# Retention's gated product ahead of its rounding, and two orders in the first block, in a two-block model kernel

## The reference, cut to what matters

```python
# first block, HGRN2 mixer: forget gate and its running sums, attention with decays between positions
fgate = lb + (1.0 - lb) * sigmoid(f);  log_f = log(fgate)
diff = bb[:, :, :, None, :] - bb[:, :, None, :, :]
decay = exp(where(mask, diff, -inf))
att = einsum('bhtd,bhsd,bhtsd->bhts', qq, kk, decay)
x = x + concatenate([y_a, y_b, y_c, y_d]) @ w_out
# second block, both layers
o = _rms((inner + cross)) * silu(gate)            # retention, 4 chunks of 128 positions
mixed = g[:, :, 0] * o_a + g[:, :, 1] * o_b + g[:, :, 2] * o_c    # g: sigmoids of a product with h
x = x + mixed @ w_out
```

## Time and profile before

| | |
|---|---|
| median of 3 runs | 2644.86 us (2643.98 to 2648.19) |
| profiled execution | 2648.18 us, its span 2646.3 us |
| TensorE busy | 2585.7 us, 98% |
| VectorE busy | 1453.3 us, 55% |
| ScalarE busy | 678.7 us, 26% |
| GpSimd busy | 1490.1 us, 56% |
| mean granted TensorE clock | 0.994 |

### The profile page before, as it was taken

One profiled execution on the slowest core, in us unless ns is written; L12 is line 12 of the kernel. 1 busy time (PEld: TensorE's weight loads), 2 busy tenths in 40 slices (PEclk: granted clock), 3 DMA queues, 4 the chain that ended last, 5 costly groups with the idle time before them and its releaser, 6 DMA issues.

```text
span 2646.3 us, 47390 instructions
## 1 busy us (share of the span) xinstructions
PE 2585.7 (98%) x16344; PEld 2020.2 (76%) x16344; DVE 1453.3 (55%) x2031; ACT 678.7 (26%) x1258; POOL 1490.1 (56%) x945
## 2 busy tenths in 40 slices
PE   8989999998999999999999999999999999999999
PEld 5768888876777677777888887777677777888887
DVE  7866555455467648764443434467648764443434
ACT  3452000034134435431200002134435531100002
POOL 4666666655544454456666666544454456566664
PEclk9999999999999999999999999999999999999999
DMA  4213332323211122223233333311122223322332
GB/s 161 67 46 112 95 94 91 93 80 108 88 57 37 48 92 64 72 73 103 89 93 95 95 95 109 95 58 37 48 92 64 72 78 97 95 91 92 95 95 95
DMA packets 72439, 222.56 MB, mean 84 GB/s; under 512 B 9312, under 2 KB 12256, under 8 KB 72288
## 3 DMA queue, kind: packets, MB, share of 16 engines
q1 hardware_dynamic: 72000, 220.46, 27.2%
q10 hardware_dynamic: 288, 0.04, 0.0%
HBM read 218.37 MB, written 2.10 MB: 83 GB/s over the span
## 4 chain that ended last, share of the span: by engine, by line
PE 90%; DVE 4%; DVEq 2%; issue 2%; DMA 1%; POOL 1%; ACT 0%; SPq 0%; ACTq 0%; POOLq 0%
PE acc L501 79%; PE bank L501 9%; DMA raw<-in_w_pg 1%; POOL w_lo L363 1%; PE bank L1098 0%; DVEq L1582 0%; DVE rw_bon L1136 0%; DVEq L1675 0%; DVE rw_SCB L1136 0%; DVE z_rw L1136 0%; DVE y_lo L1136 0%; DVE m_ta L1264 0%; DVE xg_lo L1230 0%; SPq L315 0%; DMA bs<-in_bs 0%
## 5 line engine op out<-in xcount | busy, mean ns | idle before, releaser
L363 POOL TENSOR_TENSOR w_lo<-raw,w_hi 128x1024 fp32r<-128x1024 f32 (+3 forms) x438 | 964.7, 2202 | 302.8 <-PE acc L501 274.1
L356 POOL TENSOR_SCALAR w_hi<-raw 128x1024 fp32r<-128x1024 f32 (+3 forms) x438 | 435.7, 995 | 663.5 <-PE acc L501 562.5
L501 PE MATMUL acc<-xg_hi,w_hi 128*128 128x512 f32 x2208 | 588.4, 403 | 14.0 <-issue 8.1
L501 PE MATMUL acc<-xg_lo,w_hi 128*128 128x512 f32 x2208 | 582.0, 400 | 0.0
L501 PE MATMUL acc<-xg_hi,w_lo 128*128 128x512 f32 x2208 | 580.4, 399 | 0.0
L501 PEld LDWEIGHTS acc<-xg_hi,w_hi 128*128 128x128 f32 x2208 | 408.5, 188 | 133.0 <-issue 40.2
L501 PEld LDWEIGHTS acc<-xg_lo,w_hi 128*128 128x128 f32 x2208 | 414.4, 189 | 103.1 <-issue 4.8
L501 PEld LDWEIGHTS acc<-xg_hi,w_lo 128*128 128x128 f32 x2208 | 411.4, 188 | 99.3 <-issue 0.5
L1967 ACT ACTIVATE ffn_act<-ffn_t 128x512 f32<-128x512 f32 x100 | 63.3, 633 | 775.0 <-DVEq L1196 619.5
L1136 DVE TENSOR_TENSOR x<-x,acc 128x512 f32<-128x512 f32 x104 | 71.4, 687 | 319.0 <-PE acc L501 318.5
L501 PE MATMUL acc<-hid_hi,w_hi 128*128 128x512 f32 x656 | 182.7, 396 | 3.7 <-POOL w_lo L363 1.6
(11 more groups left out here) (349 smaller groups left out, 2792.8 us busy)
## 6 DMA issues: line engine op xcount, KB each, us to landing
raw<-in_w_up SPq DMA_DIRECT2D x132, 512.0 KB, 3.6
raw<-in_w_down SPq DMA_DIRECT2D x48, 512.0 KB, 3.6
raw<-in_w_gate SPq DMA_DIRECT2D x48, 512.0 KB, 3.6
raw<-in_w_ret SPq DMA_DIRECT2D x32, 512.0 KB, 3.6
raw<-in_w_rw SPq DMA_DIRECT2D x28, 512.0 KB, 3.6
raw<-in_w_o SPq DMA_DIRECT2D x48, 256.0 KB, 2.6
raw<-in_w_in SPq DMA_DIRECT2D x18, 512.0 KB, 3.7
raw<-in_w_down SPq DMA_DIRECT2D x24, 384.0 KB, 3.0
```

The costliest lines, as they stand in the source:

```text
L356: nc.gpsimd.tensor_scalar(w_hi[:, s, 0:n], raw[:, s, 0:n], 1.0, 0.0, ALU.mult, ALU.add).then_inc(w_half[s], 1)
L363: nc.gpsimd.tensor_tensor(w_lo[:, s, 0:n], raw[:, s, 0:n], bits(w_hi[:, s, 0:n]), ALU.subtract).then_inc(w_split[s], 1)
L501: return nc.tensor.matmul(o, a, b, start=first, stop=last, skip_group_check=shared)
```

## The change

Three moves, no operation added to the mathematics. In the first block `take(2, 1)` stands right behind `take(2, 0)`, and where it stood there is a drain. At level 3 the three roundings stand ahead of `decays(4)` instead of behind it. In the retention, `branch(2n + 1)` stands behind the product with the root, ahead of the product with the gate's silu and of the rounding; its own drain takes the place of the one that stood there.

```diff
             zf = z[:, 8:10, :]
-            take(2, 0, zf)
+            for s in range(2):
+                take(2, s, zf)
             dve.wait_ge(s1["ea"], 1)
...
             v.tensor_scalar(lp[0], lp[0], 8.0, None, ALU.mult)
-            take(2, 1, zf)
+            dve.drain()
...
+                if 0 < lev < 3:
+                    decays(lev + 1)
                 if 0 < lev < 4:
-                    decays(lev + 1)
                     for j in ((), (2,), (3, 0, 1))[lev - 1]:
                         splitted(y_hi[:, j, :], y_lo[:, j, :], z[:, (0, 1, 4, 5)[j], :])
                         dve.drain()
                         dve.sem_inc(y_ready, 1)
+                if lev == 3:
+                    decays(4)
...
                     tt(rt["o"][:], rt["o"][:], rt["sq"][:])
-                    dve.drain()
+                    branch(2 * n + 1, O, mixed[:, 2 * n + 1, :])
                     after(s3, "silu", n)
                     tt(rt["o"][:], rt["o"][:], rt["gs"][:])
                     dve.drain()
                     splitted(tile_of(y2_hi, 0, 4, n), tile_of(y2_lo, 0, 4, n), rt["o"][:])
-                    branch(2 * n + 1, O, mixed[:, 2 * n + 1, :])
                     say(s3, "done")
```

## The result

| | before | changed |
|---|---|---|
| median, us (runs on the same chip) | 2646.96 (7: 2643.98 to 2652.08) | 2654.79 (7: 2648.15 to 2656.29) |
| span of the profiled execution, us | 2646.3 | 2651.4 |

The ratio is 1.0027, 95% interval 1.0017 to 1.0036: 7.8 us slower by the medians. The forecast was +5.2 (2650), range 2641 to 2655. The profiled spans differ by 5.1. Where those 5.1 lie is read by following one matmul after another through both traces. "Last part of y" is the second of the two late waits of the first block (0.94 long in both traces), "sums of the keys" the last products with `headones` ahead of the retention, "feed-forward" the first matmul on `hid_hi` in the layer.

The account below looks back on a forecast made before the run. TensorE, busy 98% of the span, was taken as the bound, so only its waits matter. Terms -2.9 (takes) + 0.7 (decays) - 0.2 (n = 0) + 7.6 (n = 1 and 2) = +5.2, added to 2644.86: 2650, range 2641 to 2655.

Parts of the forecast that it names:

- The case on the slower side: Rival: the clock falls to 1.2 GHz behind the four new waits at `kz`, 1.5 each; +11, 2656; chance 0.15.
- The largest term: Retention, n = 1 and 2, both layers: VectorE loses the memory port to GpSimd, `kz` comes late; +7.6.
- The takes: First block, two takes in a row: slot (1,3) starts earlier, gain shared with VectorE's; -2.9, bounds -1.4 and -4.8.
- bound of -4.8: Best end of the takes term: the 3.31 wait and the slow clock behind it, about 1.5, both go.
- what is late next: First block, takes: VectorE, which TensorE next meets at 91.69, waiting 1.36 for `take(5, 0)`.
- The decays: First block, level 3: 1.4 won at the fourth `y_ready`, about 2.1 lost at level-5 scores through ScalarE's corners; +0.7.
- the upper bound: Worst end of the decays term, +2.2: decays stretched by GpSimd, which starts its pooling on the same `y_ready`.
- Retention, n = 0: Both layers: the 2.95 wait ahead of the slot only moves behind it, to `kz`; -0.1 each.
- The bound of +1 each: Worst end of the retention term at n = 0, in each of the two layers.
- Retention, n = 1 and 2: Both layers: roundings fall behind GpSimd's `w_hi` and `w_lo`, TensorE waits 2.0 and 1.8 for `kz`; +7.6, lower bound 0.
- The clock in the retention: No change taken for the n = 0 waits; none for the new waits of 1.8 to 2.0, up to 1.5 each otherwise.
- the waits of 2.95 simply go: Rival: n = 0 waits vanish with their slow clock and `kz` comes earlier; -12, 2632.5; chance 0.03.

Follow-up runs that it names:

- the run that took the corners ahead: Kernel before with decays behind roundings, and ScalarE's level-4 corners and key copies ahead of its level-6 small exponentials: 2644.96, ratio 0.9991.
- the product alone: Kernel before with only the retention edit, the gated product moved up in all chunks, first block unchanged: 2658.77, ratio 1.0049.
- The filler run: Kernel before plus one unused product of 0.69 reading PSUM, behind the product with the root at n = 1 and 2, nothing moved: 2653.74, ratio 1.0025.
- the run with roundings out of PSUM: Kernel before with the retention edit, finished output for n = 0 to 2 written to a PSUM bank that both roundings read: 2651.01, ratio 1.0013.
- the one with only chunk 0 deferred: Kernel before with takes in a row, decays with corners first, and only chunk 0's silu product and roundings moved behind `kz` of chunk 1: 2644.40, ratio 0.9991.
- the two kernels with all parts that gained: Kernel before with takes, decays with corners first, and silu product and roundings behind the next chunk's `kz`: 2639.84; also with the sigmoid ahead of the silu: 2634.23.

## Why the prediction was right, step by step

The measured change, +7.8, lies in the forecast's own direction and is half as large again as its +5.2. The time, 2654.79, is only 0.2 inside the range, and of the 4.8 between it and the 2650 some 2.1 is the starting point: the forecast was added to a median of 2644.86 from three runs, and seven runs give 2646.96. The case on the slower side, 2656, was nearer. The largest term was right in its mechanism; that the whole came so near has some luck in it, as follows.

**The takes: -2.9 forecast, -2.97 measured** (less 0.17 of the start), and -3.8 by the run with this edit alone. The size is right in part by luck. It was the middle between TensorE's gain, taken as 3.3, and VectorE's, taken as 2.4. TensorE's was 4.9, since the half speed behind the wait went too (the prediction had this in its bound of -4.8 only), less 1.85 for a wait that was not foreseen. `take(2, 1)` came early and slot (1,3) at 57.40. But "what is late next" was named as slot (0,6), and it was slot (0,4) first: it needs `take(3, 0)`, which on VectorE is behind the polynomial and ran at 64.22, while TensorE was ready at 63.2. The scan pair then took 3.14 instead of 5.17, so that VectorE was some 3.0 ahead, not 2.4, when slot (0,6) needed it.

**The decays: +0.7 forecast, +1.38 in the trace of the changed kernel, +1.0 by the waits of the run with the edit alone; its median (+0.95) can't be told from nothing.** The win of 1.4 and ScalarE as what is late next are confirmed, the latter by the run that took the corners ahead. Undersized is the term behind it. The corners ran at 155.30 in the changed kernel, which is 1.66 later than at 153.64 though TensorE was 3.14 ahead: 4.8 late, not 4.0. One part of the 0.8 is the pooling of GpSimd, which starts on the same `y_ready`: the pair of decays took 2.13 instead of 1.29. The prediction had this as the upper bound and not in the sum. The wait of 0.59 at level 4, which comes of the same decays, was not named at all; without it the term is right to 0.1.

**Retention, n = 0: -0.1 each forecast, -0.5 each by the waits** (2.46 and 2.44 for 2.95). The step is right in kind, the wait only moved from the slot to `kz`. What stood behind `w_lo` was not the product (0.76) but the high rounding, as before: 2.63 at 1003.19. The prediction missed that the early slot calls GpSimd's next rounding earlier: with the product alone the low rounding then took 1.13 and the wait was 3.65 instead of 2.95, +0.7, while in the changed kernel that low rounding ran at 1005.89, ahead of `w_hi` at 1006.63, in 0.69. The edit of n = 0 alone costs +2.8. Its trace shows 0.4 in layer 0 and 1.7 in layer 1: the wait is 0.7 longer in both, and the half speed behind it cost 2.6 in both by the passes, where it had cost 2.7 and 1.5. The bound of +1 each came from no row.

**Retention, n = 1 and 2: 2.0 and 1.8 forecast, 1.94 and 1.74, 1.93 and 1.73 measured; 7.3 in all for 7.6.** This was the largest term, and it stood on a start that differed from GpSimd's by 0.01. At n = 1 of layer 0 the first encounter went the other way than taken: VectorE won it (0.69). The second one was lost by 0.01 all the same, as the prediction had said it might be either way; in the other three cases GpSimd won both (1.57 or 1.58, then 2.71). The filler run, with two cases of each outcome, and the run with roundings out of PSUM show the port to be the cause. The Trainium skill, "SBUF — State Buffer", section "Who interferes with whom", has VectorE contend where both of its inputs are in SBUF, and not where at most one is, outside its two-port modes; the run above agrees (0.69 inside a `w_lo` of 2.39). That whoever issues first has the port for the whole instruction is a little too strong for these rows. When the product with `rt_gs` had won at 1028.26 with 0.69, the 1.05 of `w_hi` became 1.60: it stood for 0.55, not 0.69, so VectorE let go some 0.14 ahead of its end.

**The clock in the retention: 0 forecast, about +2.8 measured** (+0.9 and +1.9). This is the term that was missing: the sum of the others as measured, -2.97 + 1.38 - 1.0 + 7.3 = +4.7, is the forecast's +5.2 within 0.5, and the rest up to 7.5 is clock. Over the first block and the retention together the clock cost only some 1.2, since the -2.97 holds the 1.6 that the first block got back. The prediction's rival case had it behind all of the new waits with 1.5 each; it came behind one of the two new ones a layer, with 1.7. That case tied the fall to a length between 1.36 and 2.95. The runs show that within this range the length does not decide: 1.93 and 1.73 were not followed by half speed in one place, and were in another; with 1.85 ahead of slot (0,4) the changed kernel and the one with only chunk 0 deferred kept their clock, and the two kernels with all parts that gained did not. What decides it, no run shows.

**The rivals.** That the waits of 2.95 simply go was given 0.03, and didn't happen; the reason against it was right (VectorE has the same operations ahead of `kz`), and taking these operations away, by deferring them, is what made them go.

## What to carry to other kernels

An operation that is moved up doesn't only delay the next one: it shifts all that follow against the other engine that shares the port, and hundredths then decide over 2 us each. So look for the stretch of the loop in which nobody waits for VectorE, and put there what is long or apt to be stretched; then it may be stretched. A wait that is repaired at one chunk of a loop can come back at the next, since the engines then meet elsewhere: here 2.95 at n = 0 became 2.65 at n = 1. So repair all chunks, and look at the next one ahead of counting the gain. And where a wait goes, look at the clock behind it too: a wait of 3.31 cost 4.9 here.

## What the runs showed of the hardware

Two starts in the same hundredth of a microsecond go either way: VectorE kept its 0.69 at 1028.26 and, with the filler, at 2031.71; at 1054.81 GpSimd kept its 1.05. With GpSimd 0.01 or 0.02 ahead, VectorE's low rounding took 2.92 and 2.88. A `w_lo` that lost to it was 0.6 longer (2.95), so GpSimd lost 0.6 where VectorE loses 2.2. An operation of VectorE with an input in PSUM ran at full speed inside a `w_lo` and did not lengthen it.

TensorE's clock fell to 1.2 GHz (0.50) behind waits of 1.73 to 3.65 and stayed at 2.4 GHz behind others of 1.73 to 2.32, in the same places of the program; a fall cost 1.7 us behind most waits of about 2. Single executions of the kernel before lie between 2643.98 and 2652.08 beside the changed one; falls that come in one execution and not in the next (as near 592) are a part of this, how large a part was not measured.
